# Order of the two token tiles' sigmoids, square roots and residuals in the embedding stages of a two-part transformer kernel

## The reference

```python
h = h + rms_norm(y, norm_post[i])
e = p[i] @ ple_w[i]
g = jax.nn.sigmoid(h @ ple_gate[i])
h = h + rms_norm(g * e, ple_norm[i])
```

## Time and profile before

| what | value |
|---|---|
| three runs | 1112.50, 1114.26, 1117.62 us; median 1114.26 |
| profiled execution | 1116.43 us, of which the span from first to last instruction is 1114.6 |
| TensorE's mean granted clock | 0.995 of full speed |
| busy | PE 96%, PEld 79%, POOL 64%, ACT 49%, DVE 44% |
| the chain that ended last | PE 82%, DVE 7%, ACT 6%, issue 2%, POOL 2% |

### The profile page before, as it was taken

The page is one execution under the profiler, slowest core; times in us unless marked ns, Lnnn a source line. Parts: engine busy times, 40 slices in busy tenths (PEclk is TensorE's granted clock), DMA queues, the critical chain, the costliest instruction groups (busy, mean ns, idle before and its releaser), DMA issues.

```text
span 1114.6 us, 20361 instructions
## 1 busy us (share of the span) xinstructions
PE 1066.1 (96%) x8602; PEld 881.2 (79%) x8602; DVE 494.0 (44%) x676; ACT 544.7 (49%) x870; POOL 715.9 (64%) x446
## 2 busy tenths in 40 slices
PE   9999999999999999999998999899999988999897
PEld 8788888999889879998885445598977776777675
DVE  2125176231236956355138358445465342223433
ACT  7437365444456855455432233221325457468834
POOL 6976459998857699998860017310146756896863
PEclk9999999999999999999999999999999999999999
DMA  9561455555546645555565243200014544543241
GB/s 372 208 234 62 133 161 179 189 190 188 185 139 205 190 151 188 189 188 190 186 201 181 95 151 132 76 4 4 4 59 134 197 138 156 166 157 127 95 147 52
DMA packets 45865, 167.31 MB, mean 150 GB/s; under 512 B 5616, under 2 KB 5872, under 8 KB 45456
## 3 DMA queue, kind: packets, MB, share of 16 engines
q1 hardware_dynamic: 43328, 156.97, 42.0%
q0 software_dynamic: 2448, 9.05, 2.6%
HBM read 164.95 MB, written 1.05 MB: 149 GB/s over the span
## 4 chain that ended last, share of the span: by engine, by line
PE 82%; DVE 7%; ACT 6%; issue 2%; POOL 2%; DMA 0%; SPq 0%; DVEq 0%; ACTq 0%
PE psum L434 27%; PE psum L471 19%; PE psum L685 15%; PE psum L2187 5%; PE psum L446 3%; PE psum L244 1%; PE psum L2336 1%; POOL ring_r L771 1%; ACT high_r L935 1%; PE psum L1957 1%; DVE arena L1711 1%; PE psum L2254 1%; PE psum L207 1%; PE psum L2414 1%; PE psum L2075 1%
## 5 line engine op out<-in xcount | busy, mean ns | idle before, releaser
L771 POOL TENSOR_TENSOR ring_r<-ring,high_r 128x512 fp32r<-128x512 f32 (+1 forms) x366 | 637.1, 1770 | 170.6 <-ACT high_r L935 159.0
L935 ACT CAST high_r<-ring 128x1024 fp32r<-128x1024 f32 x246 | 253.8, 1049 | 193.1 <-DMA ring<-w 192.3
L471 PE MATMUL psum<-x_high,high_r 128*128 128x256 f32 x640 | 183.0, 286 | 2.8 <-DVE x_low L308 2.8
L471 PE MATMUL psum<-x_low,high_r 128*128 128x256 f32 x640 | 181.7, 284 | 0.0
L471 PE MATMUL psum<-x_high,ring_r 128*128 128x256 f32 x640 | 181.6, 284 | 0.0
L657 DVE TENSOR_TENSOR arena<-arena 128x512 f32<-128x512 f32 x32 | 50.8, 1588 | 182.8 <-ACT arena L633 182.7
L471 PEld LDWEIGHTS psum<-x_high,high_r 128*128 128x128 f32 x640 | 123.4, 193 | 4.1 <-issue 2.5
L471 PEld LDWEIGHTS psum<-x_low,high_r 128*128 128x128 f32 x640 | 123.5, 193 | 0.5
L471 PEld LDWEIGHTS psum<-x_high,ring_r 128*128 128x128 f32 x640 | 123.4, 193 | 0.0
L434 PE MATMUL psum<-ring,arena 128*128 128x512 f32 x256 | 113.4, 596 | 2.1 <-DVE arena L1562 2.1
L434 PE MATMUL psum<-high_r,x_high 128*128 128x512 f32 x256 | 102.3, 400 | 1.7 <-DVE x_low L304 1.6
(11 more groups left out here) (347 smaller groups left out, 1817.5 us busy)
## 6 DMA issues: line engine op xcount, KB each, us to landing
ring<-w SPq DMA_DIRECT2D x288, 512.0 KB, 3.3
row<-rows POOLq DMA_DIRECT2D x14, 512.0 KB, 5.7
arena<-relt SPq DMA_DIRECT2D x2, 1536.0 KB, 11.5
h<-x SPq DMA_DIRECT2D x1, 1024.0 KB, 5.0
arena<-lora POOLq DMA_DIRECT2D x2, 512.0 KB, 6.9
out<-h SPq DMA_DIRECT2D x2, 512.0 KB, 2.6
con<-consts SPq DMA_DIRECT2D x1, 529.0 KB, 4.7
arena<-pT POOLq DMA_DIRECT2D x2, 256.0 KB, 3.5
```

The source lines that it names most:

```text
L471: ins = nc.tensor.matmul(out, a, b, start=(k == 0 and q == 0), stop=(k == KT - 1 and q == 2))
L771: ins = nc.gpsimd.tensor_tensor(low(m)[:, part], raw(m)[:, part], read(high(m))[:, part], ALU.subtract)
L935: nc.scalar.copy(high(m), raw(m)).then_inc(high_made, 1)
```

## The change

On ACT, in both embedding stages, the sigmoid of token tile 1 is issued ahead of both square roots: the root of tile 0 now comes behind it, ahead of the wait for tile 1's product and its square, and the root of tile 1 behind the loop. On DVE the reciprocal and the residual of tile 0 (now in a function `token_added`) move behind the product and the gain of tile 1, and ahead of tile 1's sum and variance; those of tile 1 stand at the end as before. No operand, shape or semaphore count changes, and PE's, SP's and POOL's programs stay as they are.

```diff
--- before.py
+++ after.py
@@ -1230,9 +1230,11 @@
                     else:
                         used(act, tile + 2)
                     nc.scalar.activation(ge[:, t, HALF:D], psum[:, 6 + t, :], ACT.Sigmoid).then_inc(gate_act, 1)
+                    if t == 1:
+                        tail_roots(i, 1, 0, 2 * NT + NT * e_n + 1)
                     act.wait_ge(ge_ready, 3 * e_n + 2 + t)
                     square_half(ge[:, t, HALF:D], 1, t, e)
-                    tail_roots(i, 1, t, 2 * NT + NT * e_n + t + 1)
+                tail_roots(i, 1, 1, 2 * NT + NT * e_n + 2)
 
             out_norm(6, W_OUT_A, 0)
             embed(7, W_PLE0, 0, T_H6)
@@ -1800,21 +1802,29 @@
                 dve.wait_ge(ge_ready, 3 * e_n + 1)
                 nc.vector.tensor_tensor(posted[:, :, 0:HALF], ge[:, :, 0:HALF],
                                         g_[:, 0:HALF].unsqueeze(1).broadcast_to([P, NT, HALF]), ALU.mult)
+                at = lambda t: slice(2 * i + t, 2 * i + t + 1)
+
+                def token_added(t):
+
+                    dve.wait_ge(tail_root, 2 * NT + NT * e_n + t + 1)
+                    settle(nc.vector.reciprocal(rstd[:, at(t)], root[:, at(t)]))
+                    for c in range(2):
+                        hl = slice(c * HALF, (c + 1) * HALF)
+                        nc.vector.scalar_tensor_tensor(out=h[:, t, hl], in0=posted[:, t, hl], scalar=rstd[:, at(t)],
+                                                       in1=h[:, t, hl], op0=ALU.mult, op1=ALU.add).then_inc(h_token, 1)
+
                 for t in range(NT):
-                    k = slice(2 * i + t, 2 * i + t + 1)
+                    k = at(t)
                     dve.wait_ge(gate_act, 3 * e_n + 2 + t)
                     nc.vector.tensor_tensor(ge[:, t, HALF:D], psum[:, 2 + t, :], ge[:, t, HALF:D], ALU.mult).then_inc(ge_ready, 1)
                     dve.wait_ge(ge_ready, 3 * e_n + 2 + t)
                     settle(nc.vector.tensor_tensor(posted[:, t, HALF:D], ge[:, t, HALF:D], g_[:, HALF:D], ALU.mult))
+                    if t == 1:
+                        token_added(0)
                     dve.wait_ge(part_sq, 4 * e + 3 + t)
                     settle(nc.vector.tensor_tensor(ss[:, k], pss[e][:, 0, t:t + 1], pss[e][:, 1, t:t + 1], ALU.add))
                     nc.vector.tensor_scalar(var[:, k], ss[:, k], 1.0 / D, EPS, ALU.mult, ALU.add).then_inc(tail_var, 1)
-                    dve.wait_ge(tail_root, 2 * NT + NT * e_n + t + 1)
-                    settle(nc.vector.reciprocal(rstd[:, k], root[:, k]))
-                    for c in range(2):
-                        hl = slice(c * HALF, (c + 1) * HALF)
-                        nc.vector.scalar_tensor_tensor(out=h[:, t, hl], in0=posted[:, t, hl], scalar=rstd[:, k], in1=h[:, t, hl],
-                                                       op0=ALU.mult, op1=ALU.add).then_inc(h_token, 1)
+                token_added(1)
 
             out_gain(6, W_OUT_A, 0, "norm_post0")
             dve.wait_ge(h_ready, 6)
```

## The result

| | before | after |
|---|---|---|
| median | 1114.90 us (1112.50 to 1117.62, 7 runs) | 1120.25 us (1118.23 to 1123.73, 7 runs) |
| ratio | | 1.0032, 95% interval 1.0016 to 1.0047 |
| profiled execution | 1116.43 us, span 1114.6 | 1118.23 us, span 1116.4 |
| mean granted clock of the profiled execution | 0.995 | 0.989 |

The kernel is slower by 0.32%, which is 3.6 us of 1114.9, with an interval from 1.8 to 5.2. The forecast was 2.0 slower. The two medians stand 5.35 apart, 0.48%, just beyond the ratio's interval; where the difference between the two figures comes from is not known here, and the text goes by the ratio. By it the forecast's 1114.26 becomes 1117.8, where 1116.3 was forecast; the median of 1120.25 by itself lies above the upper end of the range, 1119.4.

A forecast was written before the change was run, and what follows sets the result against it. PE, busy for 96% of the span, was taken as the bound, with waits at both embedding stages' ends. First stage 1.2 plus second 0.8 made 2.0 us later, 1114.26 to 1116.3 as a median; range 1113.0 to 1119.4.

The forecast's parts named there:

- The path in the first stage: First embedding stage: tile 0's residual, on the path, ends 1.5 us later; tile 1's stays hidden behind the clock hold.
- The last stage: Second embedding stage: removed sigmoid load gives nothing, tile 0's residual joins the path; ends 0.8 us later.
- B: Last stage, tile 1's sigmoid to the end of the last residual: forecast 6.0 us, where it was 5.2.
- The stores: End of the last stage: tile 0's store is through before tile 1's starts at 1113.2.
- what PE makes of it: First stage, tile 0's last transposes to the end of the clock hold: 1.2 us later, bounds -0.2 to 3.4.
- A: PE's last gate product in the first stage to the next projection's first product; forecast took 1.2 us later there.
- the middle: Next projection's first product to tile 1's sigmoid in the last stage, instructions unchanged; no added time in the forecast sum.
- Rival (a): Both embedding stages: all four table loads are on the path, 5.1 us faster, 1109.1; chance 0.04.
- Rival (b): First stage: half clock lasts until the hold is over, up to 3.4 us later there, 1118.5; chance 0.09.
- Rival (c): Next projection: half clock reaches its first products, 9.2 us slower in all, 1123.5; chance 0.03.

The follow-up runs named there:

- four traces with the first stage changed and the old hold: The change, 1.0032; the change in the first embedding stage only, +2.0 us; only ACT's reorder, +3.5; only DVE's, +3.2; 14 small products stay behind tile 0's transposes.
- second stage alone: The change made in the second embedding stage only, against the kernel before: +0.4 us (-1.3 to 2.2).
- DVE's order alone: DVE's new order with ACT's old one and all four table loads per stage, against the kernel before: +3.2 us (1.6 to 4.9).
- ACT alone: ACT's new order with DVE's old one, two table loads fewer per stage, against the kernel before: +3.5 us (1.9 to 5.1).
- hold cut to 4 products: First stage changed, 4 small clock-keeping products in place of 14 behind tile 0's transposes, against the kernel before: -2.3 us (-3.6 to -1.1).
- kernels with the hold ahead: First stage changed, 14 small products ahead of tile 0's transposes, 6 behind, against before: -2.2 us; the same plus an early root-table load in the last stage: -2.0.

## Why the prediction was right

**The path in the first stage.** Tile 0's residual was forecast 4.39 behind PE's end and came at 4.04: the gain took 1.01 where the row of before gave 1.28 beside POOL, and I had bounded it by 0.69 and 1.28; the settling took 0.03 where I had 0.13. The hold ended 1.2 later by forecast; in the trace, tile 1's transposes start 8.93 behind PE's end, where it was 8.15, so 0.8. That tile 1's residual would stay hidden behind the hold held in the four traces with the first stage changed and the old hold. In the kernel before I took it as hidden too, from one trace; where the clock did not fall (second stage alone), tile 1's transposes start at 916.43, ahead of the residual's end at 917.04, and take 1.32 in place of 1.04: there hold and data end nearly together.

**The last stage.** Forecast 0.8 later and 6.0 long; it is 5.96, 0.74 later. That the removed load would give nothing there and that tile 0's residual would take its place is shown by the kernel with DVE's order alone: it has all the loads and a B of 5.83.

**The stores.** The two stores do not meet, as forecast: the first two rows below are two separate bursts (375 and 207 GB/s on average over the rows), and nothing moves in the third row, behind the last residual's end at 1113.38.

```profile
1112.00:1113.30 1.30, 0.00 (x0) 0.00 (x0) 1.30 (x2) 0.00 (x0) 0.00 (x0) 0.50 0.92 375
1113.30:1115.00 1.70, 0.00 (x0) 0.00 (x0) 0.09 (x1) 0.00 (x0) 0.00 (x0) 0.50 0.51 207
...
1113.50:1114.00 0.50, 0.00 (x0) 0.00 (x0) 0.00 (x0) 0.00 (x0) 0.00 (x0) 0.50 0.00 0
```

**The size.** The sum was 2.0; measured are 3.6 (1.8 to 5.2), so the 2.0 lies inside the interval, and nothing has to be missing. In the two profiled executions the changed places give 0.78 + 0.74 = 1.5. If 3.6 is taken as it stands, the rest has to lie in the clock, and there my sum had two gaps. First, the term "what PE makes of it", 1.2 in the first stage: I took the half clock in the trace of before as a property of the kernel, and it is one of its two cases. Without it A is 9.12, so that an execution of before that escapes the fall loses 2.1 to 2.5 by the change, not 0.8. My bounds (-0.2 to 3.4) moved the clock in the kernel after only, never in the one before. Second, I put the middle at nothing in the forecast and had half clock there only in a rival; 6.8 us of it go with a middle 1.5 longer in the traces. The clocks of all runs point the same way: 0.9927 on average in 93 runs of before, 0.9904 in 7 runs of the change, and 0.9915, 0.9903 and 0.9907 in the three kernels with a changed first stage and the old hold. Across the runs of one kernel, 0.001 of mean clock goes with 0.6 us (a line fitted within the kernels), so 0.0023 is 1.4 us. By this estimate the clock accounts for two thirds of the 2.1 between 1.5 and 3.6, and partly for what A has already counted. That the change causes it is argued from these averages and not shown by a trace.

**The rivals.** Rival (a), the loads as the path, falls: ACT alone has them out and is 3.5 slower. Rival (b), the half clock until the hold is over, did not occur with the old hold; the clock rose within it in all four traces. It did occur with the hold cut to 4 products. Rival (c), half clock in the next projection, did not occur where I had placed it, since the clock was back at 1.00 before 919; but 3.42 us of half clock came in the products behind the wait for POOL. The prediction had no case for that, so it is in part luck that the sum still came out within the interval. What stays open is how much of the middle's 3.35 is due to the change. The kernels with the hold ahead have the longest middles of all in their traces (192.18 and 192.23) and still the higher mean clocks over their runs, so one trace's middle says little. By mean clocks, a changed first stage with the old hold goes with a lower clock (0.9908 in 39 runs of four kernels, against 0.9927), and with the hold ahead or cut to 4 products it is that of before again. Why is open: the length of PE's idle time alone does not explain it.

## What to carry to other kernels

Instructions that only keep an engine busy for the sake of its clock are themselves on the path as soon as the data behind them comes earlier: shorten or move them together with the change that brings the data, and measure that alone as well, so that the two gains can be told apart. Taking loads or switches out is worth only what lies on the path, and a reorder pays with what it moves: here 1.4 us of residual that had run beside PE's products. Before a stretch with a fallen clock is used as a baseline, look at a second trace of a kernel that is the same in that stretch, and see how fast the traced execution was among its kernel's runs.

## What the runs showed of the hardware

- The granted clock behind the same wait of PE differs from one execution to another. With the same instructions up to there, and PE idle for 1.24 and 1.02 us, the clock fell in the trace of before (0.51 in 912 to 915.5) and stayed at 1.00 in the one with the second stage changed. In the middle, behind 3.25 and 3.31 idle, it was 1.00 in one and 0.50 in the other. Runs of the kernel before in one session differ by up to 8.0 us (1112.57 to 1120.56), and 0.6 us go with each 0.001 of mean clock.
- A table load costs 1.28 us with the next activation 0.01 behind it, after as before (905.94 to 907.23). The drain of about 1.38 that the Trainium skill, "ScalarE: Activation LUTs", adds under "What ACT_TABLE_LOAD costs" appears in none of these traces; its rule to batch by table set, in "Table sets: the hidden batching unit", did here what it says to the number of loads, two fewer in each stage, while the time became 0.32% longer.
- VectorE's gain of 128x512 took 1.01 us (906.68 to 907.69) where POOL was busy until 907.14, between 0.69 without POOL and 1.28 with it.
- In the middle, 6.8 us of half clock go with 1.5 us of length and 13.6 us with 3.4 to 4.7, a quarter to a third of the half clock's own duration.
